# Index tiles that multiply the unnormalised residual, and the third front tile's steps at other turns of the logits loop

## The chip, the core and the metric

The kernel runs on one core of a Trainium2 chip. The metric is the device time of one execution in microseconds (us). TensorE is called PE (its weight loads PEld), VectorE DVE, ScalarE ACT, GpSimd POOL, and SP is the engine that issues the DMAs.

## What is computed

Two layers over 512 tokens of width 1024, in float32, and a last norm. Each layer reads the residual through a norm with a gain per feature:

```python
def rms_norm(x, gain):
    y = xf * lax.rsqrt(jnp.mean(xf * xf, axis=-1, keepdims=True) + NORM_EPS)
    return y * gain

def hybrid_mixer(h, w_in, ...):
    proj = h @ w_in            # h is rms_norm(residual, norm_mix[l])
    (qkv_a, z_a, a_a, b_a, qkv_b, q_i, k_i, w_i, g_a, g_b) = split_cols(proj, IN_SIZES)
    ...                        # gated delta rule over 8 heads: y_a
    q_i = apply_rope(q_i, cos_i, sin_i)
    k_i = apply_rope(k_i, cos_i, sin_i)
    y_b = dsa_attention(q_b, k_b, v_b, q_i, k_i, w_i) @ w_out_dsa
    merged = sigmoid(g_a) * y_a + sigmoid(g_b) * y_b
    return merged @ w_o

for l in range(DEPTH):
    h = h + hybrid_mixer(rms_norm(h, norm_mix[l]), ...)
    h = h + swiglu(rms_norm(h, norm_ffn[l]), w_gate_up[l], w_down[l])
return rms_norm(h, norm_final)
```

The norm is one factor per token (the root of the mean square) and one per feature (the gain). The indexer's scores are w_i times relu(q_i . k_i), summed over eight small heads; the best 128 keys of each query are attended to. a_a and b_a give decay and beta of the delta rule.

## The kernel before

**Layout.** Everything lies transposed: features on the 128 partitions, tokens (512) along the free axis, so the residual `h` is eight rows (k = 0 to 7) of 128x512. Each dense product of a weight tile (1024x128, eight 128x128 blocks) is made of three matmuls per block, since x and w are split in a high and a low part: x_hi w_hi, x_hi w_lo, x_lo w_hi. A tile is thus 24 products. Weights come in half tiles (units u) through a ring of six buffers; ACT makes w_hi (a rounding copy, L493), POOL makes w_lo (w_raw minus w_hi, L410), PE signals `s_tile` after each half tile, and only then is the buffer loaded again. Which unit ACT and POOL make after which tile is written out by hand (`w_hi_after`, `w_lo_after`). The order of work on every engine is the order of the program text; semaphores with named steps (`Steps`) tie the engines together.

**A layer on PE** (L1244 on): `index`, five tiles (four of q_i, one with k_i, w_i, a and b), into the two banks `dense`; then the front of the first pair of heads, eight tiles (v, k, q, z of head 0, then of head 1), woven into the logits of the indexer; then four pairs of heads of the delta rule with the next front's products as filling, eight heads of attention, the merge, w_o, and the feed-forward network (44 up tiles, 22 down tiles).

**The norm before the index tiles.** ACT squares the eight rows (L507), DVE sums rows 1 to 6 into row 0 (`sum_squares`, L823), and PE's `stats` (L1285) multiplies rows 0 and 7 with ones to get the token sums as columns. DVE makes var (L832), ACT the root, DVE the reciprocal (L834) in `rms_col`, and PE's `spread` (L1309) lays it out over all partitions in bank 3. Then `rms` on DVE (L837) makes the normalised rows y0 to y7 from h, gain and bank 3, ACT makes xn_hi (`rms_hi`), and DVE and POOL make xn_lo (rows 0, 2, 4, 7 and rows 1, 3, 5, 6). The index tiles wait for these row by row.

At the end of a layer the last down products come row by row: DVE adds each bank to the residual (L1235), ACT squares the row, DVE sums.

**The index stage.** For each tile j ACT makes two w_hi, copies the bank to `ix0` and with the halves of the heads swapped to `ixs` (four copies of 32 partitions, two for the last tile); DVE makes the rotary (three operations). After tile 4 PE turns `ix0` round (`w_tr`), which yields w_col and ab_col, from which DVE and ACT make the decay (a chain of small operations) while PE does two front tiles.

**The logits loop** (L1343 on PE, L549 on ACT, L915 on DVE) has 24 turns u, eight heads for three blocks of queries: PE one small matmul, ACT a relu, DVE an accumulation into `left`. PE waits for the relu of four turns ago, ACT for the accumulation of two turns ago. PE does 24 dense products (front tile 2) at turn 4 and eight at each of turns 16 and 20 (front tile 3). The front tiles of q, k and v pass through a short convolution: ACT scales the bank into `conv_acc` (tap), DVE adds three shifted multiples (t0, t1, t2), ACT makes tanh, DVE silu. A front tile m may be written to its bank only when t2 of tile m - 2 is done (`bank_free` in `front`).

Of the kernel before, what the change touches and what calls it, by code (L numbers as in the profile page):

```python
# [22 lines left out]
P = 128  # L23
F32 = mybir.dt.float32
F32R = mybir.dt.float32r
ALU = mybir.AluOpType
# [85 lines left out]
def hybrid_trunk(nc, x_t, w_tiles, vecs_in, mats_in, rope_in, out_t):  # L112
    with ExitStack() as ctx:
# [52 lines left out]
        cos_a, sin_a, cos_i, sin_i = (rope[:, j, :] for j in range(4))  # L166
# [9 lines left out]
        irl = [sb(f"irl_{j}", [SEQ], at=slot(45 + j)) for j in range(2)]  # L176
        w_col = sb("w_col", [NC, IH], at=slot(47))
# [90 lines left out]
        s_in = sem_of("constants_landed")  # L268
# [25 lines left out]
        def two_of(*names):  # L294
# [3 lines left out]
        rms_v = steps("rms_dve", [f"sum{k}" for k in range(1, KD - 1)] + ["var", "rstd", "y0", "y1"]  # L298
                      + ["lo0", "y2", "y3", "lo2", "y4", "y5", "lo4", "y6", "y7", "lo7"])
# [100 lines left out]
        def _(pool):  # L400
# [65 lines left out]
            def xn_lo_of(turn):  # L466

                for k in POOL_LO:
# [4 lines left out]
            for l in range(DEPTH):  # L473
                xn_lo_of(l)
# [8 lines left out]
        def _(act):  # L483
# [29 lines left out]
            def rms_hi(turn):  # L513
                for k in ks:
# [222 lines left out]

            for k in ks:
                act.wait_ge(s_x[k // 2], 16)
                square(k)  # L740
            act.wait_ge(s_in, 32)
            rms_root(0)
            w_hi_through(LEAD - 2)
            for l in range(DEPTH):
                rms_hi(l)
# [59 lines left out]
                rms_root(l + 1)  # L805
                w_hi_after(l, last)


        @block.vector
        def _(dve):  # L810
# [26 lines left out]
            def rms(turn, gain0):  # L837
                stats(turn)
                for k in ks:
                    stt(sq[:, k, :], h[:, k, :], vec[:, gain0 + k:gain0 + k + 1], bank[3][:], ALU.mult, ALU.mult).then_inc(rms_v.step(f"y{k}"), 1)  # L840
                    if k in (1, 3, 5, 7):
                        mine = k if k == KD - 1 else k - 1
                        dve.wait_ge(rms_a.sem, rms_a.after(turn, f"hi{mine}"))
                        tt_(xn_lo[:, mine, :], sq[:, mine, :], xn_hi[:, mine, :].bitcast(F32), ALU.subtract).then_inc(rms_v.step(f"lo{mine}"), 1)
# [8 lines left out]
            def index(l):  # L853
                for j in range(5):
# [901 lines left out]
```

## Time and profile before

| | us |
|---|---|
| median of three runs (2496.06 to 2500.11) | 2496.38 |
| the profiled execution, whole | 2497.91 |
| its span, first to last instruction | 2496.1 |
| PE busy | 2383.4 |
| DVE busy | 1194.4 |
| ACT busy | 1033.5 |
| POOL busy | 1180.3 |
| mean granted clock of PE | 0.985 |

The span is from the first to the last instruction of the profiled execution. Busy times are sums over the span; a matmul's end is modelled, so that matmuls that follow each other overlap in the listing: what a product takes is the distance from its start to the next one's. "Idle before" is the time in which an engine waited, with the engine that ended the wait.

### The profile page before, as it was taken

Reading aid. Unit: us, or ns where it says so; the run is one execution under the profiler, and the core shown is the slowest. Engines: PE = TensorE matmul, PEld = TensorE weight load, DVE = VectorE, ACT = ScalarE, POOL = GpSimd, SP = SyncE. Lnnn points to the kernel's source line nnn. Section 1 sums busy time; section 2 is a strip of 40 time slices with the busy share of each in tenths; the row PEclk is TensorE's granted clock in tenths of the full one; section 3 lists DMA queues with packets and bytes.
Section 4 is the critical chain, followed back from the end, with each engine's and each line's share of the span. In section 5 each row is a group of like instructions: output and inputs, shape, how many; then the busy total and the mean of one; then the engine's idle time right before and its main releaser. Section 6 shows DMA issues by size and latency. Waiting matters only on the chain.

```text
span 2496.1 us, 31779 instructions
## 1 busy us (share of the span) xinstructions
PE 2383.4 (95%) x12324; PEld 1985.0 (80%) x12324; DVE 1194.4 (48%) x2236; ACT 1033.5 (41%) x1989; POOL 1180.3 (47%) x856
## 2 busy tenths in 40 slices
PE   6899999999999999999988999999999999999998
PEld 5688887888878888888866888877888788888886
DVE  4676676554542344440156775765544423444402
ACT  5455455355542333332264454444545423333322
POOL 4273563443445555554443653653433455555542
PEclk9999999999999999999999999999999999999998
DMA  3111111022223333333321111111222233333332
GB/s 133 56 50 51 39 47 39 22 72 76 76 73 97 97 92 98 96 96 97 98 65 58 39 51 47 39 35 35 76 77 72 80 97 94 95 97 96 97 97 84
DMA packets 98502, 183.35 MB, mean 73 GB/s; under 512 B 10928, under 2 KB 11056, under 8 KB 98224
## 3 DMA queue, kind: packets, MB, share of 16 engines
q1 hardware_dynamic: 98352, 181.32, 24.7%
q8 instruction: 98, 1.61, 0.3%
q14 instruction: 52, 0.43, 0.1%
HBM read 179.18 MB, written 2.10 MB: 73 GB/s over the span
## 4 chain that ended last, share of the span: by engine, by line
PE 85%; DVE 9%; POOL 2%; ACT 2%; issue 1%; DMA 0%; SPq 0%; DVEq 0%; ACTq 0%
PE bank L1249 82%; PE bank L1315 2%; DVE conv_acc L821 1%; POOL w_lo L410 1%; DVE z_act L821 1%; POOL mt_even L435 1%; POOL mt_odd L435 1%; PE bank L1537 1%; DVE decay L1020 1%; DVE ob_lo L818 1%; DVE left L821 1%; PE bank L1309 1%; DVE left L974 1%; DVE tt L818 1%; DVE best L969 0%
## 5 line engine op out<-in xcount | busy, mean ns | idle before, releaser
L410 POOL TENSOR_TENSOR w_lo<-w_raw,w_hi 128x512 fp32r<-128x512 f32 x668 | 944.6, 1436 | 1223.0 <-ACT w_hi L493 1223.0
L1249 PE MATMUL bank<-xn_hi,w_hi 128*128 128x512 f32 x1936 | 782.8, 404 | 26.0 <-DVE conv_acc L821 16.9
L1249 PE MATMUL bank<-xn_hi,w_lo 128*128 128x512 f32 x1936 | 780.7, 403 | 0.0
L1249 PE MATMUL bank<-xn_lo,w_hi 128*128 128x512 f32 x1936 | 776.7, 401 | 0.4 <-POOL xn_lo L470 0.4
L493 ACT ACTIVATE w_hi<-w_raw 128x512 fp32r<-128x512 f32 x668 | 384.2, 623 | 726.1 <-PE bank L1249 721.0
L1249 PEld LDWEIGHTS bank<-xn_hi,w_hi 128*128 128x128 f32 x1936 | 367.8, 190 | 103.1 <-DVE conv_acc L821 20.2
L1249 PEld LDWEIGHTS bank<-xn_hi,w_lo 128*128 128x128 f32 x1936 | 368.0, 190 | 72.7 <-issue 5.4
L1249 PEld LDWEIGHTS bank<-xn_lo,w_hi 128*128 128x128 f32 x1936 | 367.3, 190 | 72.9 <-issue 1.5
L818 DVE TENSOR_TENSOR residual<-residual,bank 128x512 f32<-128x512 f32 x32 | 21.9, 685 | 259.4 <-PE bank L1249 259.2
L1249 PE MATMUL bank<-mid_hi,w_hi 128*128 128x512 f32 x352 | 136.9, 389 | 0.0
L1249 PE MATMUL bank<-mid_lo,w_hi 128*128 128x512 f32 x352 | 136.9, 389 | 0.0
L1249 PE MATMUL bank<-mid_hi,w_lo 128*128 128x512 f32 x352 | 136.9, 389 | 0.0
L821 DVE SCALAR_TENSOR_TENSOR conv_acc<-bank,hconv,conv_acc 128x511 f32<-128x511 f32 x144 | 107.2, 745 | 30.4 <-ACT conv_acc L504 27.9
L504 ACT ACTIVATE t_m<-bank 128x512 f32<-128x512 f32 (+1 forms) x96 | 49.0, 558 | 141.0 <-PE bank L1315 126.8
L435 POOL TENSOR_TENSOR mt_even<-a_t,mats 128x512 f32<-128x512 f32 x64 | 85.8, 1362 | 26.1 <-DVE a_t L821 20.0
L1249 PEld LDWEIGHTS bank<-tt,p 128*128 128x128 f32 (+1 forms) x768 | 85.9, 182 | 6.4 <-ACT p L504 2.9
L818 DVE TENSOR_TENSOR f_mid<-bank,scale_ffn 128x512 f32<-128x512 f32 x44 | 30.4, 691 | 121.2 <-PE bank L1249 121.2
L818 DVE TENSOR_TENSOR tt<-tt,bank 128x256 f32<-128x256 f32 (+1 forms) x96 | 39.6, 420 | 99.0 <-PE bank L1249 98.3
L1249 PE MATMUL bank<-tt,p 128*128 128x64 f32 (+1 forms) x768 | 84.9, 263 | 0.0
L504 ACT ACTIVATE p<-bank 128x512 f32<-128x512 f32 (+1 forms) x96 | 53.2, 560 | 69.8 <-PE bank L1249 69.0
L821 DVE SCALAR_TENSOR_TENSOR f_mid<-f_gate,f_mid 128x512 f32<-128x512 f32 x44 | 78.7, 1789 | 1.5
L1249 PEld LDWEIGHTS bank<-mid_hi,w_lo 128*128 128x128 f32 x352 | 66.1, 188 | 13.7
(247 smaller groups left out, 3523.9 us busy)
## 6 DMA issues: line engine op xcount, KB each, us to landing
w_raw<-w_tiles SPq DMA_DIRECT2D x668, 256.0 KB, 2.6
residual<-x_t SPq DMA_DIRECT2D x4, 512.0 KB, 5.8
out_t<-normalised SPq DMA_DIRECT2D x8, 256.0 KB, 2.1
rope<-rope SPq DMA_DIRECT2D x1, 1024.0 KB, 10.4
mats<-mats SPq DMA_DIRECT2D x1, 768.0 KB, 7.9
vecs_all<-vecs SPq DMA_DIRECT2D x1, 133.0 KB, 8.1
```

Of the source, the lines that this page charges most:

```text
L410: nc.gpsimd.tensor_tensor(w_lo[j][:], w_raw[j][:], w_hi[j][:].bitcast(F32), ALU.subtract).then_inc(s_lo, 1)
L435: nc.gpsimd.tensor_tensor(mt[L % 2][s][:], a_t[s][:], mat4(M_LEVEL + L), ALU.mult).then_inc(gdn_g.step(f"mt{L}_{s}"), 1)
L493: nc.scalar.activation(w_hi[j][:], w_raw[j][:], ACT.Copy).then_inc(s_hi, 1)
L504: return nc.scalar.activation(dst, src, ACT.Copy, scale=scale)
L818: return V.tensor_tensor(out, a, b, op)
L821: return V.scalar_tensor_tensor(out=out, in0=a, scalar=scalar, in1=b, op0=op0, op1=op1)
L974: V.match_replace(left[t][:], best8[t][:], left[t][:], TAKEN).then_inc(top_v.step(f"take{r}_{t}"), 1)
L1020: last = V.tensor_scalar(decay[s][:, c, :], chunks(by[s])[:, c, :], hcol[:, s, 3, c:c + 1], 0.0, ALU.subtract, ALU.min)
L1249: return nc.tensor.matmul(out, lhsT, rhs, start=start, stop=stop)
L1309: last = nc.tensor.transpose(chunks(dst)[:, c, :], col[:, c:c + 1].to_broadcast([P, P]), ident)
L1315: last = nc.tensor.transpose(chunks(dst)[:, c, :], src[:, c, :], ident)
L1537: last = nc.tensor.transpose(chunks(bank[3 + q])[:, b, :], s_m[q][:, b * P:(b + 1) * P], ident)
```

## The change

For the five index tiles the factor per token is taken out of the matmul. The tiles multiply `raw_hi` and `raw_lo`, the two parts of residual times gain. The factor goes into the rows cos and sin of the indexer's rotary (`rope_i`, two DVE multiplications with the spread in bank 3) and as a column into `w_col` and `ab_col`. The raw rows are made at the start for layer 0 and beside the last down products for layer 1. Root, spread, normalised rows and xn_hi, xn_lo move behind or between the index tiles. On PE the sums of squares come after the first index tile, the spread two thirds of a tile later. The vectors are loaded first, mats after two half tiles. In the logits loop the steps of front tiles 1 and 2 come at earlier turns. Shortened:

```diff
+        raw_hi = sb("raw_hi", [KD, SEQ], F32R, at=slot(8))
+        raw_lo = sb("raw_lo", [KD, SEQ], F32R, at=slot(22))
+        rope_i = sb("rope_i", [2, SEQ], at=slot(48))
...
         @block.sync
         def _(sp):
+            sp.dma_start(vecs_all[:], vecs_in).then_inc(s_vecs, 16)
             for k in range(0, KD, 2):
                 sp.dma_start(h[:, k:k + 2, :], x_t[:, k:k + 2, :]).then_inc(s_x[k // 2], 16)
-            for dst, src in ((mats, mats_in), (vecs_all, vecs_in)):
-                sp.dma_start(dst[:], src).then_inc(s_in, 16)
             for u in range(HALVES):
+                if u == 2:
+                    sp.dma_start(mats[:], mats_in).then_inc(s_mats, 16)
...
 (POOL)
-                xn_lo_of(l)
+                for j, slots in ((2, (1,)), (3, (3,)), (4, (5, 6))):
+                    w_lo_after(l, j)
+                    xn_lo_of(l, slots)
...
 (ACT)
+            def raw_split(l, k):
+                gain = VECS * l + V_MIX + k
+                copy(raw_hi[:, k, :], h[:, k, :], scale=vecs_all[:, gain:gain + 1]).then_inc(raw_a.step(f"hi{k}"), 1)
...
                 for j in range(5):
                     tile_done(l, j)
                     w_hi_after(l, j)
+                    if j == 0:
+                        rms_root(l)
...
                     swap(ixs[j % 2], dense[j % 2], IHD // 2, P if j < 4 else IHD).then_inc(idx_a.step(f"xs{j}"), 1)
+                    rms_hi(l, {2: (0, 1), 3: (2, 3, 4, 5), 4: (6, 7)}.get(j, ()))
...
-                    if u == len(IR) // 2:
+                    if u == 8:
                         tile_done(l, T0_GDN + 2)
                         w_hi_after(l, T0_GDN + 2)
-                    if u == len(IR) - 2:
+                    if u == 10:
                         front_tanh(l, 0, 1)
+                    if u == 12:
                         front(l, 0, 2, False, split_next=False)
...
+            act.wait_ge(s_vecs, 16)
             for k in ks:
                 act.wait_ge(s_x[k // 2], 16)
+                raw_split(0, k)
+                if k % 4 == 3:
+                    w_hi_through(k // 4)
+            for k in ks:
                 square(k)
-            act.wait_ge(s_in, 32)
-            rms_root(0)
             w_hi_through(LEAD - 2)
...
                 for m in ks:
                     act.wait_ge(dn_v.sem, dn_v.after(l, f"h{m}"))
+                    if l + 1 < DEPTH:
+                        raw_split(l + 1, m)
                     square(m)
...
 (DVE)
+            def raw_low(l, k):
+                gain = VECS * l + V_MIX + k
+                dve.wait_ge(raw_a.sem, raw_a.after(l, f"hi{k}"))
+                stt(raw_lo[:, k, :], h[:, k, :], vecs_all[:, gain:gain + 1], raw_hi[:, k, :].bitcast(F32),
+                    ALU.mult, ALU.subtract).then_inc(raw_v.step(f"lo{k}"), 1)
...
             def index(l):
+                stats(l)
+                for n, name in enumerate(("cos", "sin")):
+                    tt_(rope_i[:, n, :], rope[:, 2 + n, :], bank[3][:], ALU.mult).then_inc(rms_v.step(name), 1)
...
+                    normalise(l, {0: (0, 1), 1: (2, 3), 2: (4, 5), 3: (6, 7)}.get(j, ()))
+                    xn_low(l, {3: DVE_LO[:3], 4: DVE_LO[3:]}.get(j, ()))
...
-                    for m, what in {2: [(0, "silu")], 4: [(1, "t0_")], 6: [(1, "t1_")], 8: [(1, "t2_")]}.get(u, []):
+                    for m, what in {2: [(0, "silu")], 4: [(1, "t0_")], 6: [(1, "t1_")], 8: [(1, "t2_")],
+                                    12: [(1, "silu")], 14: [(2, "t0_")], 16: [(2, "t1_")], 18: [(2, "t2_")]}.get(u, []):
...
                     tt_(h[:, m, :], h[:, m, :], bank[m][:], ALU.add).then_inc(dn_v.step(f"h{m}"), 1)
+                    if l + 1 < DEPTH:
+                        dve.wait_ge(dn_v.sem, dn_v.after(l, f"h{m}"))
+                        raw_low(l + 1, m)
                     if m >= 2:
                         sum_squares(l + 1, m - 1)
...
 (PE)
-                Dense(l, 0, T_IDX, bank_free, x_ready=x_ready).finish()
+                first = Dense(l, 0, T_IDX, bank_free, lambda m: (raw_hi, raw_lo), x_ready)
+                first.issue(3 * KD)
+                if l == 0:
+                    pe.wait_ge(s_mats, 16)
+                sums(l)
+                first.issue(2 * KD)
+                roots(l)
+                first.finish()
...
+                def x_ready(m, k, low):
+                    if m == 0 and not during:
+                        xn_ready(l, k, low)
+                return Dense(l, T0_GDN + 8 * i, 8, bank_free, x_ready=x_ready)
...
-            pe.wait_ge(s_in, 32)
-            stats(0)
```

(`sums` and `roots` are the two halves of `stats`.)

## Rows read from the trace of the kernel before

**Rows 1.** The page: busy time of PE, and the chain's shares.

```profile
PE 2383.4 (95%) x12324; PEld 1985.0 (80%) x12324; DVE 1194.4 (48%) x2236; ACT 1033.5 (41%) x1989; POOL 1180.3 (47%) x856
...
PE 85%; DVE 9%; POOL 2%; ACT 2%; issue 1%; DMA 0%; SPq 0%; DVEq 0%; ACTq 0%
```

**Rows 2.** Chain of waits in time, 0 to 140: start us, length us, what.

```profile
3.28 8.14 DMA vecs_all<-vecs
...
29.22 26.89 PE bank L1249 x108
...
59.16 11.55 PE bank L1249 x52
...
104.65 27.60 PE bank L1249 x112
```

**Rows 3.** Waits of PE, 0 to 140: total us, times, longest.

```profile
PE bank L1249 <- DMA vecs_all<-vecs: 11.5, 1, 11.5
PE bank L1249 <- DVE conv_acc L821: 8.4, 2, 7.3
PE bank L1249 <- POOL w_lo L410: 4.5, 1, 4.5
...
PE bank L1315 <- ACT ix L504: 1.9, 1, 1.9
```

**Rows 4.** Windows, PE: stretch, length, busy (count), granted clock, DMA share, GB/s.

```profile
104.60:109.20 4.60, 4.55 (x12) 0.54 0.00 0
...
1257.60:1262.40 4.80, 4.78 (x11) 0.50 0.00 0
```

**Rows 5.** Timeline of the layer boundary: start us, length us, engine, operation.

```profile
1240.15 0.69 DVE L818 TENSOR_TENSOR residual<-residual,bank 128x512 f32<-128x512 f32 x1 [108.63 <-PE bank L1249]
...
1240.88 0.63 ACT L507 ACTIVATE squares<-residual 128x512 f32<-128x512 f32 x1 [3.65 <-DVE residual L818]
...
1246.53 0.39 PE L1249 MATMUL bank<-mid_hi,w_lo 128*128 128x512 f32 x1
1251.38 2.75 PE L1249 MATMUL bank<-mats,squares 128*128 128x1 f32 x16 [4.47 <-DVE squares L818]
1254.91 1.11 PE L1309 MATMUL bank<-mats,rms_col 128*128 128x128 f32 x4 [0.78 <-DVE rms_col L834]
1257.62 0.77 PE L1249 MATMUL bank<-xn_hi,w_hi 128*128 128x512 f32 x1 [1.59 <-ACT xn_hi L504]
```

**Rows 6.** Timeline of ACT at the start and at the last index tile.

```profile
5.32 4.96 ACT L507 ACTIVATE squares<-residual 128x512 f32<-128x512 f32 x8 [2.63 <-DMA residual<-x_t]
...
16.80 2.69 ACT L493 ACTIVATE w_hi<-w_raw 128x512 fp32r<-128x512 f32 x5
...
57.30 0.60 ACT L504 ACTIVATE ix<-bank 128x512 f32<-128x512 f32 x1
```

**Rows 7.** Timeline of POOL at the start.

```profile
17.49 1.28 POOL L410 TENSOR_TENSOR w_lo<-w_raw,w_hi 128x512 fp32r<-128x512 f32 x1 [17.05 <-ACT w_hi L493]
```

**Rows 8.** Instructions writing xn_lo: ns of one, min/median/max, first and last start.

```profile
L821 DVE SCALAR_TENSOR_TENSOR xn_lo<-residual,vec,xn_hi x16: 751/1196/1197, 848.9 to 2119.3; 128x512 fp32r<-128x512 f32 x16
```

**Rows 9.** Timeline of PEld: first front tile of layer 1.

```profile
1291.16 0.19 PEld L1249 LDWEIGHTS bank<-xn_hi,w_hi 128*128 128x128 f32 x1 [0.79 <-ACT ixs L522]
```

**Rows 10.** Timeline of DVE in and behind the logits loop of layer 0.

```profile
87.23 3.65 DVE L821 SCALAR_TENSOR_TENSOR left<-irl,w_col,left 128x384 f32<-128x384 f32 x4 [0.80 <-ACT irl L560]
...
95.17 1.54 DVE L821 SCALAR_TENSOR_TENSOR left<-irl,w_col,left 128x512 f32<-128x512 f32 x2 [1.17 <-ACT irl L560]
...
102.28 2.31 DVE L821 SCALAR_TENSOR_TENSOR conv_acc<-bank,hconv,conv_acc 128x511 f32<-128x511 f32 x3
```

**Rows 11.** Timeline of PE at the end of that loop.

```profile
93.31 1.99 PE L1249 MATMUL bank<-ik,iq 64*128 64x512 f32 x8
...
96.96 0.39 PE L1249 MATMUL bank<-xn_lo,w_hi 128*128 128x512 f32 x1
```

**Rows 12.** Timeline of ACT in the loop, relu of turn 19.

```profile
92.52 0.60 ACT L560 ACTIVATE irl<-bank 128x512 f32<-128x512 f32 x1 [0.31 <-DVE left L821]
```

More of the change, by code:

```diff
@@ L165, in hybrid_trunk @@
         ident, ones = mats[:, M_ID, :], mats[:, M_ONE, :]
-        cos_a, sin_a, cos_i, sin_i = (rope[:, j, :] for j in range(4))
+        cos_a, sin_a = (rope[:, j, :] for j in range(2))
         sq = sb("normalised", [KD, SEQ], at=slot(0))
@@ L297, in hybrid_trunk @@
         rms_a = steps("rms_act", [f"sq{k}" for k in ks] + ["sqrt"] + [f"hi{k}" for k in ks])
-        rms_v = steps("rms_dve", [f"sum{k}" for k in range(1, KD - 1)] + ["var", "rstd", "y0", "y1"]
-                      + ["lo0", "y2", "y3", "lo2", "y4", "y5", "lo4", "y6", "y7", "lo7"])
+        DVE_LO = (0, 2, 4, 7)
+        rms_v = steps("rms_dve", [f"sum{k}" for k in range(1, KD - 1)] + ["var", "rstd", "cos", "sin"]
+                      + [f"y{k}" for k in ks] + [f"lo{k}" for k in DVE_LO])
+        raw_a = steps("mixraw_act", [f"hi{k}" for k in ks])
+        raw_v = steps("mixraw_dve", [f"lo{k}" for k in ks])
         POOL_LO = (1, 3, 5, 6)
@@ L464, in gdn, with xn_lo_of @@
                 stages(*STAGES[STAGES.index("w"):])
-            def xn_lo_of(turn):
-                for k in POOL_LO:
+            def xn_lo_of(turn, slots):
+                for k in slots:
                     pool.wait_ge(rms_a.sem, rms_a.after(turn, f"hi{k}"))
@@ L511, in rms_root, with rms_hi @@
                 nc.scalar.activation(rms_col[:, 1, :], rms_col[:, 0, :], ACT.Sqrt).then_inc(rms_a.step("sqrt"), 1)
-            def rms_hi(turn):
-                for k in ks:
+            def raw_split(l, k):
+                gain = VECS * l + V_MIX + k
+                copy(raw_hi[:, k, :], h[:, k, :], scale=vecs_all[:, gain:gain + 1]).then_inc(raw_a.step(f"hi{k}"), 1)
+            def rms_hi(turn, slots):
+                for k in slots:
                     act.wait_ge(rms_v.sem, rms_v.after(turn, f"y{k}"))
@@ L804, in _ @@
                         w_hi_after(l, last - 1)
[L805 removed]
                 w_hi_after(l, last)
+            rms_root(DEPTH)
         @block.vector
@@ L835, in stats, with normalise, xn_low @@
                 dve.wait_ge(rms_p.sem, rms_p.after(turn, "bc"))
[L837 to L844, printed above, removed]
+            def raw_low(l, k):
[3 more added lines that the diff above has]
+                    ALU.mult, ALU.subtract).then_inc(raw_v.step(f"lo{k}"), 1)
+            def normalise(l, slots):
+                for k in slots:
+                    stt(sq[:, k, :], h[:, k, :], vec[:, V_MIX + k:V_MIX + k + 1], bank[3][:], ALU.mult, ALU.mult).then_inc(rms_v.step(f"y{k}"), 1)
+            def xn_low(l, slots):
+                for k in slots:
+                    dve.wait_ge(rms_a.sem, rms_a.after(l, f"hi{k}"))
+                    dve.wait_ge(rms_v.sem, rms_v.after(l, f"y{k}"))
+                    tt_(xn_lo[:, k, :], sq[:, k, :], xn_hi[:, k, :].bitcast(F32), ALU.subtract).then_inc(rms_v.step(f"lo{k}"), 1)
             def rotary(steps_, turn, out, x0, xs, cos, sin, names, rows=P):
@@ L865, in ch @@
                     return small[:, k, :].rearrange("p (c h) -> p c h", c=NC)
-                V.tensor_copy(ab_col[:], chunks(bank[2])[:, :, IHD + IH:IHD + IH + 2 * NH]).then_inc(idx_v.step("ab_col"), 1)
+                tt_(ab_col[:], chunks(bank[2])[:, :, IHD + IH:IHD + IH + 2 * NH], by_token(2 * NH), ALU.mult).then_inc(idx_v.step("ab_col"), 1)
                 dve.wait_ge(idx_v.sem, idx_v.after(l, "ab_col"))
@@ L1163, in merge @@
                     dve.wait_ge(mrg_v.sem, mrg_v.after(t, f"lo{jm}"))
+            dve.wait_ge(s_vecs, 16)
+            for k in ks:
+                raw_low(0, k)
             for k in range(1, KD - 1):
                 sum_squares(0, k)
-            dve.wait_ge(s_in, 32)
+            dve.wait_ge(s_mats, 16)
             for l in range(DEPTH):
@@ L1283, in finish, with sums @@
                     self.issue(self.products - self.n)
-            def stats(turn):
+            def sums(turn):
                 for tk in range(NC):
@@ L1293, in stats, with roots @@
                 last.then_inc(rms_p.step("ss"), 1)
+            def roots(turn):
                 pe.wait_ge(rms_v.sem, rms_v.after(turn, "rstd"))
@@ L1663, in _ @@
                         down_products(m + lead, KF - 2)
-                pe.wait_ge(dn_v.sem, dn_v.after(l, "h3"))
-                stats(l + 1)
+            pe.wait_ge(dn_v.sem, dn_v.after(DEPTH - 1, "h3"))
+            sums(DEPTH)
+            roots(DEPTH)
 def layer_vectors(norm_mix, norm_ffn, conv_w, gdn_norm, a_log, dt_bias, norm_final):
```

16 lines of the change are left out of this document (9 added, 7 removed).

## The prediction

> **What bounds the kernel now.** I read the page first. PE is busy for 95% of the span and the chain that ended last lies 85% on it [rows 1]. So an edit on another engine counts only where PE waits for it, and the question is which of PE's waits the diff touches. The next view is the chain of waits over the start and the index stage of the first layer. PE does its first work at 11.5 us, waiting for the layer vectors [rows 2, 3]; it waits 4.5 us for w_lo halves of POOL, 1.9 us for ix of ACT, and 8.4 us in two waits for conv_acc of DVE, the longest 7.3 [rows 3]. The chain in order of time places them: 108 products (the index tiles) from 29.22, the first front tile from 59.16, and from 104.65, behind the hole of 7.3 us, the fifth front tile, whose bank the third's conv steps must free [rows 2]. The windows show what a hole costs behind it: in the stretches after the holes PE goes at half clock (0.50 to 0.54) for about ten products of 0.43 us, where a product at full clock takes 0.227 (48 products and four short ones in 11.55 us) [rows 2, 4]. A hole thus costs its length and 10 x 0.2 = 2.0 us. Between the layers the last down product issues at 1246.53, the 16 products of the squares at 1251.38, the spread at 1254.91 and the first index product at 1257.62, again at half clock [rows 4, 5]. Three places, then: kernel start, layer boundary, and the end of the logits loop in both layers.
>
> **1. The start (layer 0).** Removed from in front of the index tiles: squares, sums, root, spread and the normalised rows. In their place stand raw_hi on ACT and raw_lo on DVE. The vectors are issued first, which pushes x back by one issue: the squares begin at 5.32 now [rows 6], so the first split at about 6.0. ACT's row of eight squares gives 0.62 us an operation [rows 6]: four splits to 8.5. Then w_hi of the first half tile must have landed. Now the vectors stand behind 2.9 MB (x, mats) and land 8.14 us after issue, at 11.4 [rows 2]; the half tile stands behind 2.2 MB, so I take 10.2, with 9 and 11.4 as ends. w_hi takes 0.54 (2.69 for five) [rows 6], w_lo 1.28 [rows 7]: PE starts at 12.15. Tile 0 is ten slow and 14 fast products, 4.4 + 3.2 = 7.6: done at 19.75. Meanwhile ACT does four splits, a w_hi, eight squares (to 18.9) and three w_hi (to 20.6); the last sum on DVE ends at about 19.6, so the squares' products follow tile 0 without a hole. They cost 2.8 us, the spread 1.1 [rows 5], tile 1 24 x 0.227 = 5.4: done at 29.1. The spread comes 16 products after the squares' products, 3.6 us, and hides var, root and reciprocal. mats comes before the third half tile and is needed at 19.75, with 4 MB ahead of it or in it against the 3 MB of 11.4: hidden.
>
> Tiles 2 and 3: 10.9, to 40.0. Now ACT is last, because xn_hi moved between its copies: w_hi pair 1.1, ix 0.6, four swaps 2.4 (0.6 each, taken as ix), four xn_hi 2.5, w_hi pair 1.1, ix 0.6, two swaps 1.2 [rows 6] make 9.6, to 49.6; PE starts the first front tile at **49.7, not 59.16: 9.5 us**. Tile 4 is done at 45.4, so PE waits about 3 us for ix where it waits 1.9 now. xn_lo on POOL (behind the w_lo of tile 4) is done by 52.5 and is wanted at 53.5: hidden by 1 us; if not, PE waits the difference. The ends: 7.5 if the weights land at 11.4 and DVE is slowed, 11 if they land at 9.
>
> Rotary rows times the spread are two DVE operations of 0.7 us in the shade of ix0. The scaled w_col and ab_col are as small as now. One xn_lo more stands before the decay chain on DVE (0.7 to 1.2), and PE needs its cumulative product 10.9 us after the first front tile starts; most is hidden, 0.2 us a layer charged, 1 at most.
>
> **2. The boundary (layer 1).** Now DVE adds a row of the residual for every six products, 1.36 us; after the change each turn is serial: add 0.69, ACT's split 0.63 [rows 5], raw_lo 0.75 [rows 8], sum 0.6, and no other row is in between, since DVE waits inside the turn: 2.66 us. Behind that wait stand the next adds, and ACT and PE wait for these. From h0 at 1240.15 and with the first two rows without a sum, h7 comes at 1257.6 to 1258.1 and the last sum ends at about 1260.8. ACT's w_hi pair for tile 0's second half stands behind row 4 (1251.3). So PE runs 12 products at once after 1246.8, trickles through the other 12, and is at the squares' products at 1260.85: 2.8, at half clock 0.7 more, tile 1 5.4 + 0.8 for four slow products, spread 0.9 to 1.1: 1271.5 or so. With the 20.6 us of part 1 the first front tile starts at 1292.1; now it does at 1291.16 [rows 9]. **Loss 0.9 us**; ends a loss of 3 (four raw_lo or sums at 1.2 and ten slow products) and a gain of 1.5 (none of it).
>
> Here a rule of the notes can be weighed. The row shows raw_lo's twin, xn_lo from the residual and xn_hi, at 0.75 us alone and 1.20 at the median, when POOL is subtracting [rows 8]: 0.45 a meeting, which the sum uses. The Trainium skill, SBUF — State Buffer, section "Who interferes with whom", says that a VectorE instruction with two SBUF inputs and a GpSimd one that reads SBUF exclude each other for the whole instruction. By it each of the two POOL subtractions in the stretch could hold DVE for up to 1.3 us, and part 2 would lose up to 1.7 us more; the row stays far under that.
>
> **3. The third front tile.** Its w_hi goes from turn 12 to 8 of the loop, tanh1 and tap2 from 22 to 10 and 12, silu1 and the three conv steps from behind the masks into turns 12 to 18. Now the masks and silu1 stand in front of the conv steps, which take 2.31 from 102.28 on [rows 10]; PE's last free product ends its turn at 96.96 + 0.23 [rows 11]. After it the bank is free before PE asks, so the hole of 104.65 - 97.2 = 7.45 goes, and with it the ten slow products, 2.0. What is given back: DVE does 2.8 us more in the loop, with idle pieces of 0.80 and 1.17 in it [rows 10], the first of them behind the w_hi. But PE runs four logits ahead and has 16 dense products between them (two times 1.8 us); the last of its last four starts at about 94.8 [rows 11], the relu of turn 19 that it needs ends at 93.12 [rows 12]: 1.7 us of slack, against three inserted steps before that turn, 2.1, less the 0.80 that the earlier w_hi gives back. I charge 0.3, ends 0 and 2.1. **9.15 us a layer, 18.3 in both**, ends 13.5 and 18.9. What is late next: the following bank (z of tile 3) wants w_hi, tanh and one copy on ACT, 2.5 us against 5.4 of PE, so nothing. DVE's masks end later but its next work comes with tile 4.
>
> **Sum.** 9.5 - 0.9 + 18.3 - 0.4 = 26.5. The profiled execution has a span of 2496.1 and a time of 2497.91, so 2469.6 and 2471.4; its time is 1.5 above the median of the three runs, 2496.38, against which it is **2470 us**. With all ends: 7.5 - 3 + 13.5 - 2 = 16 and 11 + 1.5 + 18.9 = 31.
>
> **The rivals.** (a) The loop becomes DVE-bound: PE's last logits and tile 4 wait for the inserted steps. Against it: the 1.7 us of slack; for it: DVE works without a gap for 3.65 us from 87.23 [rows 10]. Price 2 x (2.1 - 0.3) = 3.6, and 1 a layer if tile 4 waits for the third conv step: 2476. (b) The head start is smaller: weights at 11.4, ACT late by a landing of x, and the boundary at its worst: 2 + 2 = 4, 2474. (c) The boundary keeps its clock and the loop costs nothing: 2.4 + 0.6 + 1 = 4 more gained, 2466. (d) **Slower**: each product trickle of tile 0, with its holes of 1 to 2.7 us, keeps the clock at half through all index tiles of both layers, 240 products at 0.2 us, 48 us, of which about 5 is in the sum: 2470 + 43 = 2513. It decides once more than 26.5 / 0.2 = 130 products more go at half clock. Against it: in both stretches the clock came back after about ten products [rows 4]. The Trainium skill, TensorE: Matmul & The Clock Gate, section "Part 1: The HAM clock gate", says that half clock is the idle state and sustained activity lifts it; by that the dense tiles 1 to 4 end (d). (e) The moved work doesn't come earlier (another wait holds the index tiles): 2496.
>
> **How the numbers follow.** Forecast 0.55 (own range 2465 to 2475), (a) 0.15, (b) 0.13, (c) 0.12, (d) 0.02, (e) 0.03. The range runs from the best to the worst sum of ends with a little for what is not seen further down: 2464 to 2481. A measurement here tells 0.2%, 5 us: faster 0.95, same 0.03, slower 0.02.
>
> **What would show it.** In the profile after: first dense product near 12, tile 1 done near 29, first front tile near 50, no PE wait for conv_acc of 7 us, granted clock 1.00 behind the loop; at the boundary a residual add every 2.7 us and raw_lo between, the index stage starting front tiles within 2 us of where they start now. Wrong would be a wait for landing weights past 11.4, DVE steps of 1.8 us in the raw splits, or PE waiting for relu in the last logits.

## The result, and the profile after

| | before | after |
|---|---|---|
| median, us (4 runs each, side by side) | 2498.24 | 2483.06 |
| lowest to highest | 2496.06 to 2502.14 | 2480.36 to 2486.64 |
| span of the profiled execution | 2496.1 | 2483.3 |
| mean granted clock of PE | 0.985 | 0.984 |

The ratio is 0.9937, 95% interval 0.9924 to 0.9950: 15 us faster, 12.8 us by the two profiled spans. The forecast was 2470 with 2481 as the upper end; its gain of 26.5 us came in at half. PE issues as many matmuls as before and is busy for 5.7 us more [rows 1]:

```profile
PE 2389.1 (96%) x12324; PEld 1985.6 (80%) x12324; DVE 1225.3 (49%) x2256; ACT 1042.2 (42%) x2005; POOL 1183.9 (48%) x856
```

Points on PE's timeline, in us, say where the gain is made and lost. "F" is the first product of the first front tile, "rest" the last dense products before the hole [rows 11], "kt" the first product of the delta rule behind that hole.

| layer 0 | before | after | gain so far |
|---|---|---|---|
| squares' products (behind tile 0 after) | 11.46 | 21.93 | |
| F | 59.16 | 53.39 | 5.8 |
| cumulative product of the decay | 70.18 | 67.14 | 3.0 |
| first dense product of turn 4 | 73.85 | 70.91 | 2.9 |
| logits behind it | 79.52 | 79.32 | 0.2 |
| rest | 95.23 | 97.07 | -1.8 |
| kt | 132.09 | 124.43 | 7.7 |

| layer 1 | before | after | gain so far |
|---|---|---|---|
| first residual add of the boundary (h0) | 1240.15 | 1230.02 | 10.1 |
| squares' products | 1251.38 | 1252.19 | |
| F | 1291.16 | 1284.71 | 6.4 |
| cumulative product | 1302.18 | 1298.44 | 3.7 |
| logits behind turn 4's dense products | 1311.51 | 1309.49 | 2.0 |
| rest | 1327.22 | 1328.29 | -1.1 |
| kt | 1364.20 | 1355.63 | 8.6 |

Up to kt layer 0 gains 7.7 and, from its h0 on, layer 1 loses 1.6. The other 6.7 us lie in stretches that the change doesn't touch: kt to h0 is 2.5 shorter, kt of layer 1 to the end 4.2. I come back to them.

The chain of waits over the start and index stage (start us, length us, what):

```profile
9.93 0.64 ACT w_hi L503
10.64 1.28 POOL w_lo L418
11.97 7.31 PE bank L1292 x24
19.28 2.65 issue
21.93 8.91 PE bank L1292 x32
...
52.70 4.97 DVE xn_lo L840 x3
```

PE starts at 11.97 as forecast, but the squares' products, forecast at 19.75, come at 21.93, and in front of the decay stand three xn_lo of DVE with 4.97 us. Waits of PE, 0 to 140 (total us, times, longest):

```profile
PE bank L1292 <- POOL w_lo L418: 12.0, 1, 12.0
PE bank L1360 <- ACT ix L514: 2.7, 1, 2.7
PE bank L1292 <- issue: 2.7, 1, 2.7
PE bank L1292 <- ACT irl L578: 1.3, 3, 0.5
PE bank L1292 <- DVE conv_acc L843: 1.1, 1, 1.1
PE bank L1292 <- DVE small L840: 0.9, 1, 0.9
PE bank L1292 <- DVE small L843: 0.8, 1, 0.8
PE bank L1292 <- ACT ixs L536: 0.6, 1, 0.6
```

The 7.3 us for conv_acc [rows 3] is gone. In its place stand many waits of about 1 us. What stands behind them on PE is in the windows (stretch, length, busy (count) of PE, PEld, DVE, ACT, POOL, granted clock, DMA share, GB/s):

```profile
25.00:29.00 4.00, 4.00 (x11) 3.23 (x11) 0.34 (x2) 3.04 (x6) 0.40 (x1) 0.50 0.00 0
53.40:56.40 3.00, 3.00 (x7) 2.16 (x8) 3.00 (x3) 1.11 (x2) 3.00 (x3) 0.51 0.00 0
70.90:76.60 5.70, 5.69 (x13) 4.46 (x14) 3.05 (x5) 3.55 (x8) 2.52 (x2) 0.50 0.01 3
88.00:90.20 2.20, 2.20 (x6) 1.77 (x6) 2.13 (x5) 1.01 (x3) 0.00 (x0) 0.50 0.00 0
1255.60:1261.00 5.40, 5.40 (x14) 4.24 (x15) 0.34 (x2) 3.04 (x6) 1.35 (x2) 0.50 0.00 0
1302.20:1306.00 3.80, 3.77 (x10) 3.04 (x11) 1.24 (x1) 2.79 (x6) 2.52 (x2) 0.55 0.00 0
```

At 0.50 PE goes at 1.2 GHz and a dense product takes 0.43 us instead of 0.227. Counted by the distance of starts (above 0.35 us), between start and kt and between h0 and kt of layer 1, 47 products go at half clock before and **87** after (one or two more or fewer by where one cuts): 40 x 0.2 = 8 us.

DVE and POOL at the start and at F (start, length, engine, operation):

```profile
5.46 1.28 ACT L514 ACT_TABLE_LOAD   x1 [5.46 <-DMA residual<-x_t]
...
11.21 4.27 DVE L843 SCALAR_TENSOR_TENSOR raw_lo<-residual,vecs_all,raw_hi 128x512 fp32r<-128x512 f32 x4 [0.88 <-ACT raw_hi L514]
...
15.40 6.43 DVE L840 TENSOR_TENSOR squares<-squares 128x512 f32<-128x512 f32 x6
...
18.30 7.11 POOL L418 TENSOR_TENSOR w_lo<-w_raw,w_hi 128x512 fp32r<-128x512 f32 x5 [3.37 <-ACT w_hi L503]
...
38.86 0.69 DVE L840 TENSOR_TENSOR iq<-iq,ixs 128x512 f32<-128x512 f32 x1
...
49.74 1.64 DVE L840 TENSOR_TENSOR iq<-iq,ixs 128x512 f32<-128x512 f32 x1
...
52.62 5.05 DVE L840 TENSOR_TENSOR xn_lo<-normalised,xn_hi 128x512 fp32r<-128x512 f32 x3
...
64.27 2.54 POOL L418 TENSOR_TENSOR w_lo<-w_raw,w_hi 128x512 fp32r<-128x512 f32 x2 [7.15 <-ACT w_hi L503]
...
64.45 1.16 DVE L932 TENSOR_SCALAR small<-small 128x32 f32<-128x32 f32 x1
...
65.64 1.22 DVE L840 TENSOR_TENSOR small<-small 128x32 f32<-128x32 f32 x1
```

A DVE operation with two inputs in SBUF takes 0.69 alone and 1.64 to 1.7 when it meets a POOL subtraction: 5.05 for three xn_lo. The last two lines are small steps of the decay chain. Their neighbours of the same size take 0.18 to 0.19; beside POOL's two w_lo these take 1.16 and 1.22, 2.0 us more on the chain that the cumulative product waits for. The kernel before has the same pair (1.16 at 66.22, 1.23 at 67.41), but there the chain ends before PE asks.

At the boundary a turn is 2.81 us (residual adds at 1237.29, 1240.10 and 1242.91), one raw_lo meets POOL, and PE's largest wait is 4.0 us for w_lo:

```profile
1242.91 0.68 DVE L840 TENSOR_TENSOR residual<-residual,bank 128x512 f32<-128x512 f32 x1
1244.45 1.46 DVE L843 SCALAR_TENSOR_TENSOR raw_lo<-residual,vecs_all,raw_hi 128x512 fp32r<-128x512 f32 x1 [0.86 <-ACT raw_hi L514]
...
1244.17 0.79 PE L1292 MATMUL bank<-raw_hi,w_hi 128*128 128x512 f32 x1 [4.03 <-POOL w_lo L418]
```

### The profile page after: what moved, and what is told of

It reads as the page before. It is cut to its first block, busy times and chain, and to the rows that moved or that the text cites. A ratio compares the mean times of both kernels' runs of the same rounds, so it can differ in the third digit from the quotient of the medians.

```text
span 2483.3 us, 31838 instructions
## 1 busy us (share of the span) xinstructions
PE 2389.1 (96%) x12324; PEld 1985.6 (80%) x12324; DVE 1225.3 (49%) x2256; ACT 1042.2 (42%) x2005; POOL 1183.9 (48%) x856
## 4 chain that ended last, share of the span: by engine, by line
PE 85%; DVE 9%; POOL 2%; ACT 2%; issue 2%; DMA 0%; SPq 0%; DVEq 0%; ACTq 0%
PE bank L1292 82%; PE bank L1360 1%; DVE conv_acc L843 1%; DVE z_act L843 1%; POOL w_lo L418 1%; POOL mt_even L443 1%; POOL mt_odd L443 1%; PE bank L1594 1%; DVE decay L1058 1%; DVE ob_lo L840 1%; PE bank L1354 1%; DVE tt L840 1%; DVE left L1012 0%; DVE xn_lo L840 0%; DVE best L1007 0%
## 5 line engine op out<-in xcount | busy, mean ns | idle before, releaser
L1292 PE MATMUL bank<-xn_hi,w_hi 128*128 128x512 f32 x1856 | 750.4, 404 | 3.4 <-DVE conv_acc L843 2.3
L1292 PE MATMUL bank<-xn_hi,w_lo 128*128 128x512 f32 x1856 | 748.8, 403 | 0.0
L1292 PE MATMUL bank<-xn_lo,w_hi 128*128 128x512 f32 x1856 | 745.7, 402 | 0.1
L1292 PEld LDWEIGHTS bank<-xn_hi,w_hi 128*128 128x128 f32 x1856 | 352.5, 190 | 76.4 <-issue 4.9
L1292 PEld LDWEIGHTS bank<-xn_lo,w_hi 128*128 128x128 f32 x1856 | 352.6, 190 | 69.7 <-DVE xn_lo L840 1.6
L1292 PEld LDWEIGHTS bank<-xn_hi,w_lo 128*128 128x128 f32 x1856 | 352.5, 190 | 69.6 <-issue 5.4
L1292 PEld LDWEIGHTS bank<-tt,p 128*128 128x128 f32 (+1 forms) x768 | 86.4, 183 | 6.4 <-ACT p L514 2.9
L1292 PEld LDWEIGHTS bank<-mid_hi,w_hi 128*128 128x128 f32 x352 | 66.1, 188 | 13.8
```

The lines of the kernel that those rows point to most:

```text
L1292: return nc.tensor.matmul(out, lhsT, rhs, start=start, stop=stop)
```

## The experiments

Every kernel was timed beside the kernel before on the same chip; ratios are to it. Four runs of one kernel differ by 3 to 7 us, so times tell 3 us at best, and what is below that is read from the timelines.

**The two parts apart.** e1_raw_only is the kernel after with the logits loop of before; e2_loop_only is the kernel before with the loop of after. The diff is that of e1 on ACT; on DVE silu1 and the three conv steps go back from turns 12 to 18 to behind the masks. e2 has the opposite:

```diff
-                    if u == 8:
+                    if u == len(IR) // 2:
                         tile_done(l, T0_GDN + 2)
...
-                    if u == 10:
+                    if u == len(IR) - 2:
                         front_tanh(l, 0, 1)
-                    if u == 12:
                         front(l, 0, 2, False, split_next=False)
```

> The changed kernel with the logits loop as it was before: only the raw index tiles and all that hangs on them. Theory A (each layer's head start is eaten again by half-clock products and by DVE held up beside POOL, and the loop part brings nearly all): 2494 to 2499 us, within 0.2% of before; first front tile still 5 to 6 us earlier than before in layer 0, the dense products of turn 4 at half clock, the first logits behind them within 1 us of before. Theory B (the raw part brings its 9 us in layer 0 and the loop part is smaller than forecast): 2487 to 2490.

> The kernel before with only the steps of front tiles 1 and 2 moved up in the logits loop. Theory A: 18 us gained less 2 to 4 for the longer loop, 2480 to 2484 us, as fast as the changed kernel; the hole of 7.3 us in front of the fifth front tile gone, granted clock 1.00 there. Theory B: 6 to 8 us gained, 2489 to 2492.

e1_raw_only: 2502.04 us, ratio 1.0011 [1.0002, 1.0020]. e2_loop_only: 2484.08, 0.9935 [0.9920, 0.9950], the ratio of the whole change. Both theories put e1 lower; alone, the raw tiles gain **nothing**. F of layer 0 comes 5.3 earlier there (53.91), the logits behind turn 4 0.5 later (79.97), kt at the same time (132.13). In layer 1 it loses: from h0 to kt it takes 135.4 us, before 124.1. Some 106 products go at half clock, 59 more than before, 12 us. PE's waits in it keep the old hole and have the new small ones:

```profile
PE bank L1290 <- DVE conv_acc L842: 8.4, 2, 7.3
PE bank L1358 <- ACT ix L514: 2.7, 1, 2.7
PE bank L1290 <- issue: 2.5, 1, 2.5
```

e2 has a warning for what follows. Up to turn 8 its code is that of before, and so are its waits of 0.89 and 1.12 in front of turn 4. Yet in layer 0 five products at F and eight in turn 4 go at half clock, none of them before, and the logits behind turn 4 come at 82.38 for 79.52. In layer 1 neither happens:

```profile
75.10:82.38 7.28, 7.28 (x24) 5.55 (x24) 4.16 (x6) 3.53 (x8) 2.52 (x2) 0.77 0.10 38
...
1299.98:1305.65 5.67, 5.67 (x25) 4.43 (x25) 3.04 (x5) 3.54 (x8) 2.53 (x2) 1.00 0.13 46
```

**The clock held.** e3_filled is the kernel after with 97 matmuls put into PE's waits: their results go to a bank that nobody reads, so they add nothing to what is computed. e9_loop_filled2 has 52 such matmuls in the waits of e2. In e3 there are 9 at the squares of layer 0, 16 and three times 8 in the trickle of the boundary, 12 before w_tr and 2 behind it, 3 each at the cumulative product and at the head of the loop, 4 at turn 4. Shortened:

```diff
+            def idle_products(n, dst=7):
+                for _ in range(n):
+                    mm(bank[dst][:], raw_hi[:, 0, :P], raw_hi[:, 1, :])
...
+                idle_products(12)
                 pe.wait_ge(idx_a.sem, idx_a.after(l, "x4"))
...
                     if u == 4:
+                        idle_products(4)
                         d.issue(3 * KD)
```

> The changed kernel plus matmuls whose results nobody reads, put where PE waits: before the squares' products, between the raw products of layer 1's first tile, before and after the turning of ix, before the cumulative product, the first logits and the dense products of turn 4 (some 90 products, all in holes). Nothing of the computation changes. If the half clock behind short holes is what ate the gain (theory A), the stretches behind them go at clock 1.00, each saves up to 2 us, and the time falls by 5 to 10 us against the changed kernel, to 2474 to 2479, although PE does more. If the waits themselves are what costs (theory C), the time stays or rises by 1 to 3 us: 2483 to 2486.

> The kernel before with the loop part and the unread matmuls in the holes around it, but none in turns 5 to 15 (these lengthened turns 4 to 16 from 9 to 14 us where they were tried). It is the twin of the filled raw kernel (2478.0) without the raw part. Theory A (with the clock held up the raw part is worth something): 2481 to 2484. Rival (worth nothing): 2476 to 2479.

e3_filled: 2478.0, ratio 0.9912 [0.9897, 0.9927], the lowest median of all kernels here: PE does more and the kernel is 5 us faster than after. Half-clock products fall from 87 to some 35. The windows:

```profile
25.00:29.00 4.00, 4.00 (x21) 3.26 (x21) 0.46 (x3) 3.05 (x6) 1.33 (x2) 1.00 0.02 6
...
70.90:75.50 4.60, 4.60 (x25) 3.46 (x23) 3.92 (x6) 1.74 (x6) 1.76 (x2) 1.00 0.21 57
```

The logits behind turn 4 come at 74.57, kt at 120.33, 4.1 before the kernel after. But F to the cumulative product stays 13.81 against 13.75, at full clock: that stretch is bound by something else. e9_loop_filled2: 2480.16, 0.9916 [0.9900, 0.9932], some 45 half-clock products; it lies between its two expectations. With and without the raw tiles the ratios differ by 0.0004, far inside their intervals, so with the clock held too the raw part is worth nothing that can be measured.

The same by the timelines, one trace of each kernel: the two stretches that the change touches (start to kt of layer 0, h0 to kt of layer 1), added.

| kernel | us in the touched stretches |
|---|---|
| before | 256.1 |
| e1_raw_only | 267.6 |
| e2_loop_only | 246.8 |
| after | 250.0 |
| e4_pool_waits | 243.4 |
| e3_filled | 240.9 |
| e9_loop_filled2 | 241.5 |

Without fillings the raw tiles cost 3 us here beside the loop part and 11 alone; with fillings they neither cost nor bring anything. The medians show less of this, since the stretches that nobody touched move too (see the 6.7 us below).

**The fillings inside the turns.** e6_loop_filled was e9 with one matmul more in each of turns 5 to 15:

```diff
+                    if 4 < u < 16:
+                        idle_products(1)
```

> The kernel before with the loop part, and unread matmuls in its holes: 18 before the squares' products of layer 1, 8 before and 2 after the turning of ix, 3 before the first logits, 4 before the dense products of turn 4, one in each of turns 5 to 15. Index tiles still take the normalised rows. Theory A (with the clock held up the raw part is worth its 4 to 9 us in layer 0): this one is slower than the filled raw kernel (2478.0) by 2 to 8 us, 2480 to 2484. Rival (the raw part is worth nothing even then): 2474 to 2478.

2487.92, 0.9956 [0.9941, 0.9971]: a miss. The stretch from the logits behind turn 4 (79.49) to turn 16's dense products (93.42) takes 13.9 us, where it takes 7.1 before and 8.4 in e9, the twin without these fillings. The timeline has each turn at 1.06 to 1.27 us with the filling in it:

```profile
86.25 0.91 PE L1251 MATMUL bank<-ik,iq 64*128 64x384 f32 x2
87.09 0.49 PE L1251 MATMUL bank<-xn_hi 128*128 128x512 f32 x1
```

The 11 fillings of a layer cost 5.6 us, 0.5 each, where a dense product takes 0.23. The waits that they could fill add to 1.35 us in e9 (0.51, 0.40, 0.44). A filling pays only where PE waits for longer than it takes.

**DVE beside POOL, at the sums.** e4_pool_waits holds POOL's third w_lo until the sums of squares of layer 0 are done:

```diff
-            w_lo_through(0)
+            w_lo_through(1)
+            pool.wait_ge(rms_v.sem, rms_v.after(0, f"sum{KD - 2}"))
```

> The changed kernel with POOL's w_lo of the third half tile on held back until DVE's last sum of squares of layer 0. If DVE's sums were slow because POOL subtracted beside them (6.43 us for six against 4.68 before), they end 1.5 to 2 us earlier, the squares' products start near 20.2 instead of 21.93, and 1.5 to 4 us are gained in layer 0 (the upper end if the clock then stays up): 2479 to 2482. If the cause lies elsewhere, the sums stay at 6.4 us and the time stays at 2483.

2480.32, 0.9924 [0.9908, 0.9941], inside the expectation. The six sums take 4.66 us for 6.43, the squares' products come at 20.66, the wait in front of them is 1.03 for 2.65, and they take 1.98 for 3.32:

```profile
15.90 4.66 DVE L841 TENSOR_TENSOR squares<-squares 128x512 f32<-128x512 f32 x6
...
20.66 1.98 PE L1293 MATMUL bank<-mats,squares 128*128 128x1 f32 x16 [1.03 <-issue]
```

On the timeline this one wait of POOL does nearly as much as the 97 fillings: F of layer 0 comes at 50.48 (2.9 earlier than after) and kt at 120.03 (4.4 earlier). Part of it is the clock: turn 4's products take 5.66 us for 8.41 in layer 0, and 5.66 for 7.26 in layer 1 too, whose code e4 leaves as it was.

**DVE beside POOL, at xn_lo.** e5_spread makes xn_hi and xn_lo a tile earlier (ACT after tiles 1, 2, 3, 4; DVE after 2, 3, 4); e8_pool_holds has POOL wait for DVE's third xn_lo instead:

```diff
                 for j, slots in ((2, (1,)), (3, (3,)), (4, (5, 6))):
+                    if j == 4:
+                        pool.wait_ge(rms_v.sem, rms_v.after(l, "lo4"))
                     w_lo_after(l, j)
```

> The changed kernel with xn_hi and the four xn_lo rows of DVE made a tile earlier, one or two rows behind each index tile, and only two behind the last rotary. If the three xn_lo rows that stand in front of the last rotary (5.05 us beside POOL, where 2.1 was the price) and the four xn_hi in front of the last ix are what eats the head start between first front tile and cumulative product, ix comes 1.2 us earlier, the stretch from first front tile to cumulative product falls from 13.75 to 11 or 12 us, and 2 to 4 us a layer are gained: 2475 to 2479. If it is the half clock alone that eats it, only the 1.2 us a layer show: 2480 to 2481.

> The changed kernel with POOL held back, in front of its last two w_lo of the index stage and its last two xn_lo, until DVE's third xn_lo row is done. If POOL's subtractions beside them are what makes DVE's three xn_lo rows 5.05 us long, they take 2.1 to 2.5 us, the last rotary starts 2 to 3 us earlier, the stretch from first front tile to cumulative product falls from 13.75 to 11 to 12.5 us and 2 to 4 us are gained over both layers or more: 2478 to 2481. If the rows are slow for another reason, they stay at 5 us and the time at 2483.

e5_spread: 2482.74, 0.9936 [0.9921, 0.9950], a miss. xn_lo earlier meets POOL as well: 1.70 and 1.72, and so do the rotary's operations around it (1.58 and 1.64). F to the cumulative product takes 14.3, with a wait of 1.27 for DVE's xn_lo in it. Moving the operations moved the collision. e8_pool_holds: 2481.32, 0.9921 [0.9904, 0.9939]. The time is nearly as expected, the reason isn't: three xn_lo take 1.88, but POOL's work now meets what comes next.

```profile
51.46 1.88 DVE L842 TENSOR_TENSOR xn_lo<-normalised,xn_hi 128x512 fp32r<-128x512 f32 x3
53.26 0.68 DVE L842 TENSOR_TENSOR ik<-ix,rope_i 64x512 f32<-64x512 f32 x1
53.97 1.65 DVE L842 TENSOR_TENSOR ixs<-ixs,rope_i 64x512 f32<-64x512 f32 x1
55.66 1.66 DVE L842 TENSOR_TENSOR ik<-ik,ixs 64x512 f32<-64x512 f32 x1
57.24 1.76 DVE L842 TENSOR_TENSOR xn_lo<-normalised,xn_hi 128x512 fp32r<-128x512 f32 x1
```

F to the cumulative product is 14.45, not the 11 to 12.5 expected; 1.25 of it are two waits for POOL's own xn_lo (0.55 and 0.70). What was gained lies in the clock: turn 4's dense products take 5.67 instead of 8.41.

**All together.** e7_all has the fillings, those in the turns, POOL's first wait and the spread. e10_filled_pool has the fillings and both waits of POOL; e11_filled_wait and e12_filled_holds have one of the two each.

> The changed kernel with all of it: the unread matmuls in the holes, one more in each of turns 5 to 15, POOL held back until the sums of squares, and xn_hi and xn_lo spread. If the losses are separate, their gains add up: 5 for the clock, 2.7 for POOL, 2 to 6 for the spread, 1 to 3 for the loop, partly the same microseconds: 2466 to 2473. If they are the same microseconds counted twice, 2475 to 2478.

> The changed kernel with the unread matmuls (none in turns 5 to 15) and POOL held back at both places. If clock and POOL are separate losses, 5 + 2.7 + 1 to 3 are gained against the changed kernel: 2472 to 2475. If they overlap, 2476 to 2478.

> The filled kernel with GpSimd's first wait alone (its third half tile's subtraction waits for the last sum of squares of layer 0). It separates the two waits of the kernel that had both and came out at 2482.6 instead of the 2472 to 2475 that adding the savings gave. Theory A: the first wait keeps its worth (1.5 us at the squares' products, as it was without fillings) and the second wait spoiled the sum: squares' products of layer 0 at about 21.5 to 22 instead of 23.1, first front tile near 50, time 2475 to 2477.5, below the filled kernel. Rival B: the first wait's loss is GpSimd's delay in front of the next half tiles, which the fillings no longer hide: first front tile at 51 to 52 and the cumulative product again more than 15 us behind it, time 2479 to 2483.

> The filled kernel with GpSimd's second wait alone (in each layer it waits for VectorE's xn_lo of row 4 before the weight parts behind the fourth index tile). Theory A: this wait is what cost in the kernel with both: the way from the first front tile to the cumulative product is 16 us or more in layer 0, against 13.8 in the filled kernel without it, and the time is 2480 to 2483. Rival B: this wait costs nothing and the first one did: 13.8 us or less, and 2476 to 2478.5.

| kernel | us | ratio | F, layer 0 | F to cumulative product | kt, layer 0 |
|---|---|---|---|---|---|
| after | 2483.06 | 0.9937 [0.9924, 0.9950] | 53.39 | 13.75 | 124.43 |
| e3_filled | 2478.0 | 0.9912 [0.9897, 0.9927] | 51.32 | 13.81 | 120.33 |
| e11_filled_wait | 2478.8 | 0.9922 [0.9906, 0.9939] | 50.85 | 13.82 | 119.11 |
| e12_filled_holds | 2483.01 | 0.9934 [0.9920, 0.9949] | 51.17 | 17.94 | 124.99 |
| e10_filled_pool | 2482.57 | 0.9926 [0.9911, 0.9940] | 51.66 | 16.75 | 123.81 |
| e7_all | 2487.15 | 0.9952 [0.9935, 0.9968] | 49.72 | 16.25 | 124.50 |

e7 and e10 missed. e7 has the highest granted clock of the kernels up to then (0.992) and is slower than after: 13.9 us go into turns 5 to 15, as in e6, and PE waits 2.4 us for xn_lo. e11 and e12 settle e10: POOL's second wait is what costs. Behind it POOL's own two xn_lo (rows 5 and 6) come late, PE waits for them, and 14 products go at half clock behind the waits (PE timeline, and the window):

```profile
57.45 0.50 PE L1294 MATMUL bank<-xn_lo,w_hi 128*128 128x512 f32 x1 [2.14 <-POOL xn_lo L478]
59.13 0.80 PE L1294 MATMUL bank<-xn_lo,w_hi 128*128 128x512 f32 x1 [0.70 <-POOL xn_lo L478]
...
59.10:65.20 6.10, 6.07 (x14) 4.79 (x15) 4.79 (x15) 4.86 (x9) 2.53 (x2) 0.51 0.13 46
```

That is 2.8 us of waiting, and 14 x 0.2 = 2.8 of clock; e3 has 0.6 of the one and none of the other. In e8, where F is 1.1 us later than in e12, the waits for these rows were 1.25: the earlier F comes, the less time POOL has. The first wait keeps its worth on the timeline (kt 1.2 earlier than in e3), but not in the median: 2478.8 lies between e11's two expectations, and its four runs between 2474.02 and 2481.27.

## Why the prediction was wrong in size

The mechanism of the loop part came as forecast; the gain of the raw tiles was lost to DVE steps beside POOL and to half clock behind short waits. The time came out above the range because four terms passed the ends that I gave them: part 1 (7.5 us), part 2 (a loss of 3), the decay chain (1 us a layer) and, in layer 1, the loop (2.1).

**Right.** The start (11.97 for 12.15), tile 0 done at 19.28 for 19.75, and ACT's 9.6 us from the end of tile 3 to F: its products end at 44.03, F comes at 53.39; the wait for ix is 2.73, forecast at about 3. The hole's term, 9.45 a layer, was charged at 9.15 with the loop: from "rest" to kt layer 0 gains 36.86 - 27.36 = 9.5 and layer 1 9.6. e2 shows that this part carries the whole result.

**Part 1, 9.5 forecast, 5.8 measured at F.** The squares' products were put at 19.75 and came at 21.93. The step that failed is "the last sum on DVE ends at about 19.6", which let the sums follow ACT's squares. ACT wasn't late: its squares ended at 17.70 where I had 18.9, and the table load of 1.28 us in front of its first split, which I hadn't counted, cost nothing, since ACT then waits 0.62 for the first half tile of weights. DVE was late, because it met POOL's w_lo twice: the second four raw_lo took 4.27 for the 2.74 of the first four, so the sums began at 15.40, and took 6.43 for 4.68. Without these 3.3 us the sums, which need ACT's second square at about 14.6, would have ended at about 19.3, with tile 0 (an estimate from these times). Behind the hole of 2.65 us nine products went at half clock, 1.8. Together 4.0 at the end of tile 3, against 0.2 gained at the start. e4 takes one of the two meetings out and has F 2.9 us earlier.

**From F to turn 4, 0.2 a layer charged, 5.6 and 4.4 measured.** This was the largest error: 9.6 of the 20.4 us by which the steps fell short (26.5 forecast, 7.7 - 1.6 = 6.1 measured); the others are 3.7, 2.8 and 4.5. "xn_lo hidden" and "decay chain 0.2" took xn_lo on DVE at 0.7 to 1.2. It took 1.7 three times in a row, straight ahead of the decay chain; without the 3.0 us of excess the cumulative product could have come at 67.14 - 3.0 = 64.1, before the 48 products were done. So the chain was no longer in PE's shade, and with it the 2.0 us that POOL's w_lo puts into its two small steps, hidden before. In layer 0 F to the cumulative product takes 2.7 more: 0.8 of waiting at its end, where there was none, 1.2 in six products at half clock at F, the rest in small gaps. Then come waits of 0.9 and 1.1 that were there before too, and now 13 products at half clock in turn 4, 2.7. That the new wait of 0.8 brings these is likely, not shown: with it turn 4 is slow in all four stretches without fillings (both layers of after and e1), without it in two of ten (layer 0 of e2 and of e5). e3 takes out the clock's share (F to the logits is 23.25 us there, 25.93 after, 20.36 before) and leaves the chain's. That a faster xn_lo alone shortens the chain no run shows: in e8 the collision went on to the rotary. Nor was POOL's w_lo beside the two small steps ever held back.

**Part 2, 0.9 lost forecast, 3.7 measured.** h0 to the squares' products took 22.2 us for 20.7: a turn is 2.81, not 2.66, since DVE waits 0.86 for ACT's split where I had 0.63 (from start to start the add and this wait take 1.54, raw_lo 0.67, the sum 0.60), and one raw_lo took 1.46. From there to F 32.5 for 31.25: 13 products at half clock behind the squares' products, where I had four.

**Part 3, 0.3 charged, 2.0 and 3.1 measured.** The loop is longer by this from the logits behind turn 4 to the rest. In layer 0 PE waits three times for a relu (0.51, 0.40, 0.44; before twice, 0.37 and 0.20), and behind the waits five products go at half clock at 88.05, 1.0 us; in layer 1 it is eight. That comes near rival (a), whose price was 1.8 more a layer, though it had the last logits wait. The error was to set 2.1 us of inserted steps against the slack of the last logits; the waits fall before turn 16, where PE has no dense products to give it slack:

```profile
83.43 0.91 PE L1292 MATMUL bank<-ik,iq 64*128 64x384 f32 x2 [0.51 <-ACT irl L578]
...
86.08 2.03 PE L1292 MATMUL bank<-ik,iq 64*128 64x384 f32 x4 [0.44 <-ACT irl L578]
```

**The two rules weighed.** The trace has a DVE operation at 0.69 alone and 1.68 in a meeting, 1.0 a meeting, where I had taken 0.45 from [rows 8]. The small steps of the decay chain pay the same 1.0 (1.16 and 1.22 for 0.18), though they are a sixteenth of the size. The Trainium skill, SBUF — State Buffer, "Who interferes with whom", calls the ports that VectorE shares with GpSimd an exclusive lock and says that a VectorE instruction with two SBUF inputs contends with a GpSimd one that reads SBUF. A POOL subtraction takes 1.28 us here; the measured 1.0, the same for a large and a small operation, is nearer to a wait for a whole instruction than to my row. The median of [rows 8], 1.20, belongs to meetings in other places and didn't carry over. Rival (d) didn't come: each run of dense products at half clock ended after 3 to 13 of them. The Trainium skill, TensorE: Matmul & The Clock Gate, "Part 1: The HAM clock gate", has it that activity releases the throttle; this agrees. But 40 products more went at half clock without it; the error was to charge the clock only behind holes I had listed. The same page of the Trainium skill, "A second HAM failure mode: psum-queue depth-cycling", tells of a clock that goes up and down because TensorE idles for short moments between groups of matmuls. The count of 87 against 47, and some 35 once the waits are filled, agrees; the 60 of e2, whose waits up to turn 8 are nearly those of before, show that the waits alone don't settle the count.

**The 6.7 us that no step forecast.** They are not in changed code. In the last pair of each layer's delta rule (kt to the transposes of dv) the same 516 matmuls take 86.3 and 86.4 us before, 83.8 and 83.6 after. Windows of layer 0, before and then after:

```profile
414.30:500.60 86.30, 74.75 (x516) 65.82 (x514) 51.87 (x127) 38.08 (x79) 39.44 (x31) 0.92 0.09 24
```

```profile
406.60:490.50 83.90, 73.93 (x517) 64.58 (x516) 54.20 (x127) 38.03 (x79) 40.43 (x31) 0.94 0.10 27
```

The clock is 0.92 in the one and 0.94 in the other. Most experiment kernels have 83.6 to 84.0 in both layers, but e2 in layer 1 and e6, e9 and e10 in layer 0 have 85.3 to 86.3, without a pattern in what was changed. In e3, e7, e10 and e12, all with fillings, one or two earlier pairs take 96.2 for 94.6. At the very end the 16 products of the last squares run once at half clock and once not, behind the same wait:

```profile
2482.70 3.54 PE L1249 MATMUL bank<-mats,squares 128*128 128x1 f32 x16 [3.61 <-ACT squares L507]
```

```profile
2471.37 2.10 PE L1292 MATMUL bank<-mats,squares 128*128 128x1 f32 x16 [3.62 <-ACT squares L517]
```

The granted clock there is 0.50 in the one and 0.88 in the other. So the clock falls in different places of untouched code from kernel to kernel. What sets it stays open; it gave this change some 6 us, which is luck, and without it the miss would have been larger. Open too: whether the raw part pays with another division of the subtractions between DVE and POOL. None was tried in which no two of them meet.

## What to carry to other kernels

Taking a wait away is worth what the chain behind it leaves: look up what is late next for every engine, and place the new operations against each other, not only against PE (two-input DVE operations beside POOL's subtractions took 1.7 us for 0.69, and small steps on a chain 1.2 for 0.18). Count half-clock products before and after; one long hole may be cheaper than four short ones, if each brings its own slow products. Don't lay a few such products to one wait by one trace: they also came and went where neither the code nor the waits had changed. Where a short wait can't be removed, matmuls that nobody reads may be worth having (5 us here), but not where PE isn't waiting.

## What the runs showed of the hardware

- Waits of about 1 us on PE can have half clock behind them if several lie close together: behind waits of 0.8, 0.9 and 1.1 us 13 products in layer 0 of after. They needn't: behind 0.9 and 1.1 alone turn 4's products took 5.67 us in eight stretches (both layers of before, e4 and e8, layer 1 of e2 and e5) and 7.3 in two (layer 0 of e2 and e5).
- The cost of a meeting of DVE and POOL differs by place: 1.0 for a two-input operation at F and 0.7 for raw_lo at the boundary, 0.45 by [rows 8].
- It doesn't shrink with the operation: steps of 128x32 took 1.16 and 1.22 us beside POOL's w_lo, 0.18 to 0.19 elsewhere, in the kernel before as well. The copy of the layer's vectors took 1.28 beside it, 0.23 in the kernel before.
- The same 16 products behind the same wait of 3.6 us took 3.54 and 2.10 us in two programs.
